# Modulations of the first layer by tiles of features, the first three products tile by tile, and the last modulation group by halves of columns

## The reference

```
def first_block(x, c, w_ada, b_ada, ...):
    c_act = jax.nn.silu(c)
    for i in range(DEPTH):
        mods = jnp.split(c_act @ w_ada[i] + b_ada[i], 6, axis=-1)
        sh1, sc1, g1, sh2, sc2, g2 = [m[:, None, :] for m in mods]
        u = x * (1.0 + sc1) + sh1
        ... y = gla_mixer(u, ...) or chunk_attention(u, ...)
        x = layer_norm(DEEPNORM_ALPHA * x + (1.0 + g1) * y, ...)
        u = x * (1.0 + sc2) + sh2
        y = squared_relu_mlp(u, ff_w1[i], ff_w2[i])
        x = layer_norm(DEEPNORM_ALPHA * x + (1.0 + g2) * y, ...)

def gla_mixer(u, w_in, w_gk2, b_gk, g_norm, w_out):
    proj = u @ w_in
    q, k, v, g, gk_lr = jnp.split(proj, ...)
    log_a = jax.nn.log_sigmoid((gk_lr @ w_gk2 + b_gk)) / GLA_GATE_TAU
    ... cumulated in chunks of 64 frames; q and k are scaled by its exponentials
```

## Time and profile before

| | us |
|---|---|
| median of 3 runs | 1144.07 (1142.17 to 1144.33) |
| the profiled execution, as timed | 1143.43 |
| its span in the trace | 1141.1 |
| PE busy | 1032.3 (90%) |
| DVE busy | 824.7 (72%) |
| ACT busy | 504.7 (44%) |
| all of PE's first 34.3 us | idle |

### The profile page before, as it was taken

One profiled execution on the slowest core, in us unless ns is written; L12 is line 12 of the kernel. 1 busy time (PEld: TensorE's weight loads), 2 busy tenths in 40 slices (PEclk: granted clock), 3 DMA queues, 4 the chain that ended last, 5 costly groups with the idle time before them and its releaser, 6 DMA issues. The chain is left out here.

```text
span 1141.1 us, 16510 instructions
## 1 busy us (share of the span) xinstructions
PE 1032.3 (90%) x6736; PEld 923.4 (81%) x6736; DVE 824.7 (72%) x1118; ACT 504.7 (44%) x669; POOL 64.1 (6%) x138
## 2 busy tenths in 40 slices
PE   0789988999999899868999999699999989999996
PEld 0778967899989688747898989488888879999995
DVE  4668898888779788747856556856876567777775
ACT  0464524333433644535334343354345555555553
POOL 3001110000000111100000000100000000000000
PEclk9989998999999999988999999799999999999999
DMA  9858775778778377322655555253343434555651
GB/s 340 334 197 302 276 298 196 287 291 304 283 275 320 105 289 247 129 74 74 240 189 180 195 177 197 89 170 138 111 144 116 148 130 152 200 171 186 198 172 68
DMA packets 35049, 227.91 MB, mean 200 GB/s; under 512 B 4096, under 2 KB 4224, under 8 KB 10144
## 3 DMA queue, kind: packets, MB, share of 16 engines
q1 hardware_dynamic: 25232, 167.01, 42.0%
q0 software_dynamic: 9744, 59.87, 14.0%
HBM read 225.82 MB, written 1.05 MB: 199 GB/s over the span
## 5 line engine op out<-in xcount | busy, mean ns | idle before, releaser
L1387 DVE TENSOR_TENSOR weight_lo<-weight_raw,weight_hi 128x2048 fp32r<-128x2048 f32 (+3 forms) x187 | 361.4, 1936 | 115.1 <-ACT weight_hi L991 115.0
L416 PE MATMUL ps<-act_hi,weight_hi 128*128 128x256 f32 x1400 | 354.2, 291 | 11.4 <-ACT gla_q L995 5.6
L991 ACT ACTIVATE weight_hi<-weight_raw 128x2048 fp32r<-128x2048 f32 (+2 forms) x168 | 299.9, 1786 | 128.9 <-PE ps L416 97.3
L416 PE MATMUL ps<-act_lo,weight_hi 128*128 128x256 f32 x1400 | 349.0, 287 | 0.0
L416 PEld LDWEIGHTS ps<-act_hi,weight_hi 128*128 128x128 f32 x1400 | 274.4, 196 | 23.0 <-issue 13.4
L416 PEld LDWEIGHTS ps<-act_lo,weight_hi 128*128 128x128 f32 x1400 | 274.7, 196 | 3.4 <-issue 1.0
L416 PE MATMUL ps<-act_hi,weight_lo 128*128 128x256 f32 x1400 | 186.8, 283 | 0.0
L416 PEld LDWEIGHTS ps<-act_hi,weight_lo 128*128 128x128 f32 x1400 | 175.5, 191 | 0.2
L1407 DVE SCALAR_TENSOR_TENSOR ada_acc<-ada_raw,c_act,ada_acc 128x2048 f32<-128x2048 f32 x42 | 98.6, 2349 | 10.2 <-DMA ada_raw<-ada 8.8
L416 PE MATMUL ps<-weight_hi,mlp_lo 128*128 128x512 f32 x256 | 101.8, 398 | 0.0
L416 PE MATMUL ps<-weight_hi,mlp_hi 128*128 128x512 f32 x256 | 101.6, 397 | 0.0
(11 more groups left out here) (311 smaller groups left out, 1263.0 us busy)
## 6 DMA issues: line engine op xcount, KB each, us to landing
weight_raw<-weights SPq DMA_DIRECT2D x144, 1024.0 KB, 5.0
ada_raw<-ada POOLq DMA_DIRECT2D x48, 1024.0 KB, 6.5
weight_raw<-weights SPq DMA_DIRECT2D x23, 512.0 KB, 3.6
row_g<-ln_rows POOLq DMA_DIRECT2D x4, 512.0 KB, 5.4
row_b<-ln_rows POOLq DMA_DIRECT2D x4, 512.0 KB, 7.7
att_bias<-rel_bias POOLq DMA_DIRECT2D x16, 128.0 KB, 3.5
square<-ada_rows POOLq DMA_DIRECT2D x3, 512.0 KB, 3.8
dev<-x_in SPq DMA_DIRECT2D x1, 1024.0 KB, 10.5
```

What stands on the lines that cost most here:

```text
L416: return e.matmul(o, a, b, start=start, stop=False, skip_group_check=True)
L991: e.activation(weight_hi[h][:, 0:size], weight_raw[r][:, 0:size], ACT.Copy).then_inc(hi_full[h], 1)
L1387: ins = e.tensor_tensor(weight_lo[h][:, c], weight_raw[r][:, c], weight_hi[h][:, c].bitcast(F32), ALU.subtract)
```

## The change

On the host (`_ada`), group 0 is stored by tiles of output features: chunk `f` holds all 1024 input features by 256 columns, the shift and scale of tile `f`. `first_input` on DVE runs eight accumulations of 256 columns per chunk and puts between them the reading of the modulations of the tile before (`mods_in`) and its `act_lo` (`residue`); the first three `split_lo` stand between tiles. PE sums a tile with one-column matmuls (`first_mods`), runs `gk` from tile 4 on and `q0` from tile 6 on, and then all of `q1` into a bank of its own, ahead of the gate products. ACT forms each tile's `act_hi` and `square` (DVE formed half of the latter before). SP no longer waits to load `x`, and loads the first weights after tiles 0, 2 and 4.

Groups 2 and 5 (the last of each layer) come by halves of columns: the first four chunks complete the 1024 columns of the MLP's scale, the last four those of its gate row; each chunk is two operations of 1024 columns. The scale then needs 20 chunks instead of 24: one chunk fewer after the third gate product, none before the mixer's output product, and four more in the first MLP. Both MLPs' gate rows are summed after block 8 instead of block 1.

```
-USES = ["m0", "gk", "q0", "q1", "k0", "k1", "v0", "v1", "v2", "v3", "g0", "g1", "g2", "sh0", "g3", "ra0", "ra1", "sc0"]
-USES += [f"up0_{i}" for i in range(2)] + ["rb0", "rb1"] + [f"up0_{i}" for i in range(2, 16)] + ["m3"]
+USES = ["gk", "q0", "k0", "k1", "v0", "v1", "v2", "v3", "g0", "g1", "g2", "sh0", "g3", "ra0", "ra1", "sc0"]
+USES += [f"up0_{i}" for i in range(9)] + ["rb0", "rb1"] + [f"up0_{i}" for i in range(9, 16)] + ["m3"]
...
-ACC_FREE = (0, 0, 1, 4, 7, 8)
-ADA_V, ADA_G = (1, 2, 2, 1), (2, 2, 2, 0)
+SUMS = ["sh0", "ra0", "ra1", "sc0", "rb0", "rb1", "m3", "sh1", "rc0", "rc1", "sc1", "rd0", "rd1"]
+ACC_FREE = (0, 0, 0, 3, 6, 7)
+ADA_V, ADA_G = (1, 2, 2, 1), (2, 2, 1, 0)
...
-            e.wait_ge(ada_used, 3)
...
-                    e.wait_ge(ada_used, 5 + j)
+                    e.wait_ge(ada_used, (1, 3, 5)[j])
...
-            def pair(one, two, ready, share=3, hook=None):
...
+            def first_mods(f):
+                e.wait_ge(ada_used, f + 1)
+                if f >= 2:
+                    e.wait_ge(u_mods, f - 1)
+                for x in range(2):
+                    last = e.matmul(ps[:, 6 + f % 2, x:x + 1], ada_acc[:, (2 * f + x) * P:(2 * f + x + 1) * P],
+                                    ones_sq[:, 0:1], start=(x == 0), stop=True, skip_group_check=True)
+                last.then_inc(u_summed, 1)
+            def first_chunk(j, outs, wide, tiles):
+                at = products(j, outs, act_hi, act_lo, KT, wide, True, False)
+                e.wait_ge(hi_full[j], 1)
+                e.wait_ge(lo_full[j], 1)
+                for k in tiles:
+                    e.wait_ge(lo_in, LO_U + k + 1)
+                    for n in range(len(outs)):
+                        o, one, two, three, start = at(n, k)
+                        mm(o, *one, start=start)
+                        mm(o, *two)
+                        last = mm(o, *three)
+                return last
...
-                if w >= 2:
-                    e.wait_ge(*emptied(w))
-                e.wait_ge(ada_used, KT * (group + 1))
+                e.wait_ge(*emptied(w))
+                e.wait_ge(ada_used, KT * (group + 1) - (4 if group % 3 == 2 else 0))
...
-            mods_of("m0", 0, 0, 16)
-            e.wait_ge(*emptied(W["q0"]))
-            pair((0, work_tiles(W["gk"], 1), P), (1, work_tiles(W["q0"]), 256), lambda k: (lo_in, LO_U + k + 1), share=6)
+            first = ((0, work_tiles(W["gk"], 1), P, 4), (1, work_tiles(W["q0"]), 256, 6))
+            for f in range(KT):
+                first_mods(f)
+                for j, outs, wide, begin in first:
+                    if f >= begin:
+                        first_chunk(j, outs, wide, range(f) if f == begin else (f - 1,))
+            for j, outs, wide, _ in first:
+                first_chunk(j, outs, wide, (KT - 1,)).then_inc(chunk_done, 1)
+            first_chunk(2, [(q1_ps[:, n, :], 4) for n in range(2)], 256, range(KT)).then_inc(chunk_done, 1)
             e.wait_ge(*evacuated(W["gk"]))
             e.wait_ge(w2_in, 16)
             for h in range(GLA_H):
                 last = e.matmul(gate_ps[:, h, :], g_w2[:, h * P:(h + 1) * P], g_gk[0:GLA_RANK, :], start=True, stop=True,
                                 skip_group_check=True)
             last.then_inc(gate_done, 1)
-            project(2, W["q1"])
...
-                if row:
-                    mod_row(row[0] + "0", row[1], D)
-                    mod_row(row[0] + "1", row[1], D + HALF)
                 for i in range(2, n_blocks - 1):
                     down(i - 2)
                     project(up_chunk(m, i), up_use(m, i))
+                    if row and i == 8:
+                        mod_row(row[0] + "0", row[1], D)
+                        mod_row(row[0] + "1", row[1], D + HALF)
...
-            split_hi(0)
-            split_hi(1)
-            e.wait_ge(scale_in, 1)
             e.wait_ge(x_arrived, 16)
             for k in range(KT):
                 scale, bias = norm_scale[:, 0, k:k + 1], mod(0, 0, k)
+                e.wait_ge(u_mods, k + 1)
                 e.activation(act_hi[:, k, :], dev[:, k, :], ACT.Identity, bias=bias, scale=scale).then_inc(hi_in, 1)
-                if k % 2:
-                    e.activation(square[:, k, :], dev[:, k, :], ACT.Identity, bias=bias, scale=scale).then_inc(hi_in, 1)
-            split_hi(2)
+                e.activation(square[:, k, :], dev[:, k, :], ACT.Identity, bias=bias, scale=scale).then_inc(hi_in, 1)
+                if k in (2, 4, 6):
+                    split_hi(k // 2 - 1)
...
-            evacuate(2, W["q1"], g_q[:, 2:4, :], halves(W["q1"]), GLA_DK ** -0.5)
+            e.wait_ge(chunk_done, 3)
+            e.activation(g_q[:, 2:4, :], q1_ps, ACT.Copy, scale=GLA_DK ** -0.5).then_inc(q1_in, 1)
...
-                    e.wait_ge(c_done, 1)
+                    e.wait_ge(u_summed, KT)
                     if ACC_FREE[n // KT]:
                         e.wait_ge(mods_summed, ACC_FREE[n // KT])
-                    ins = e.tensor_scalar(a, ada_raw[slot][:, :], c_act[:, 0:1], None, ALU.mult)
                 else:
                     e.wait_ge(ada_used, n)
-                    ins = e.scalar_tensor_tensor(out=a, in0=ada_raw[slot][:, :], scalar=c_act[:, k:k + 1], in1=a,
-                                                 op0=ALU.mult, op1=ALU.add)
+                if n // KT % 3 == 2:
+                    half = a[:, k // 4 * D:(k // 4 + 1) * D]
+                    parts = [(half, raw[:, x * D:(x + 1) * D], 2 * (k % 4) + x) for x in range(2)]
+                else:
+                    parts = [(a, raw[:, :], k)]
+                for x, (to, of, row) in enumerate(parts):
+                    if x:
+                        e.wait_ge(dve_step, own.of(ins))
+                    if row == 0:
+                        ins = e.tensor_scalar(to, of, c_act[:, 0:1], None, ALU.mult)
+                    else:
+                        ins = e.scalar_tensor_tensor(out=to, in0=of, scalar=c_act[:, row:row + 1], in1=to, op0=ALU.mult,
+                                                     op1=ALU.add)
...
-            def input_u():
...
+            def first_input():
+                def mods_in(f):
+                    b = VEC["b_ada"] + f
+                    e.wait_ge(u_summed, f + 1)
+                    n = own.of(e.tensor_tensor(mods[0][:, f:2 * KT:KT], ps[:, 6 + f % 2, 0:2], vec[:, b:b + KT + 1:KT],
+                                               ALU.add))
+                    e.wait_ge(dve_step, n)
+                    e.tensor_scalar(norm_scale[:, 0, f:f + 1], mod(0, 1, f), 1.0, None, ALU.add).then_inc(u_mods, 1)
+                def residue(f):
+                    e.wait_ge(hi_in, 2 * f + 2)
+                    e.tensor_tensor(act_lo[:, f, :], square[:, f, :], act_hi[:, f, :].bitcast(F32),
+                                    ALU.subtract).then_inc(lo_in, 1)
+                e.wait_ge(c_done, 1)
+                for f in range(KT):
+                    slot = f % N_ADA_RING
+                    to = ada_acc[:, 2 * f * P:2 * (f + 1) * P]
+                    raw = ada_raw[slot][:, :].rearrange("p (k n) -> p k n", k=KT)
+                    e.wait_ge(ada_full[slot], 16 * (f // N_ADA_RING + 1))
+                    n = own.of(e.tensor_scalar(to, raw[:, 0, :], c_act[:, 0:1], None, ALU.mult))
+                    for k in range(1, KT):
+                        e.wait_ge(dve_step, n)
+                        ins = e.scalar_tensor_tensor(out=to, in0=raw[:, k, :], scalar=c_act[:, k:k + 1], in1=to,
+                                                     op0=ALU.mult, op1=ALU.add)
+                        if k < KT - 1:
+                            n = own.of(ins)
+                            if f and k == 2:
+                                mods_in(f - 1)
+                            if f and k == 6:
+                                residue(f - 1)
+                    ins.then_inc(ada_used, 1)
+                    if f in (3, 5):
+                        split_lo(f // 2 - 1)
+                mods_in(KT - 1)
+                split_lo(2)
+                residue(KT - 1)
...
-            for _ in range(KT):
-                ada_chunk()
-            split_lo(0)
-            split_lo(1)
-            mods_of("m0", 0, 0, 16)
-            e.wait_ge(*evacuated(W["m0"]))
-            e.tensor_scalar(norm_scale[:, 0, :], mod(0, 1), 1.0, None, ALU.add).then_inc(scale_in, 1)
-            e.wait_ge(scale_in, 1)
-            e.wait_ge(x_arrived, 16)
-            input_u()
-            split_lo(2)
+            ada_at[0] = KT
+            first_input()
...
-            for _ in range(3):
-                ada_chunk()
...
-                for n in range(2):
-                    gate_half(f"{row}{n}", 2 * m + 1, n)
...
-                    if fill and i == n_blocks - 2:
+                    if i == 8:
+                        for n in range(2):
+                            gate_half(f"{row}{n}", 2 * m + 1, n)
+                    if fill and (i == n_blocks - 2 or i in (2, 4, 6, 10)):
...
```

(3 more changed lines are left out.)

78 lines of the change are left out of this document (19 added, 59 removed).

## The result

The changed kernel takes 1154.13 us, median of 4 runs (1152.73 to 1154.62); the kernel before, beside it, 1143.55 (1142.17 to 1144.33). The ratio is 1.0086, 95% interval 1.0063 to 1.0109: slower by 10.6 us in the medians, 9.7 in the profiled executions (span 1150.8 against 1141.1). The forecast was 1149.3 with a range of 1143.5 to 1155.0, slower at 0.77. The direction and the stated range held; the size was forecast at half, and 1154.13 lies outside the range that the forecast gave its own sum, 1146.5 to 1152.5.

A forecast was written before the change was run, and what follows sets the result against it. PE, busy 90% of the time, was taken to be held in the first stage by when the gate products are read. 6.6 - 1.3 - 0.4 + 0.3 = +5.2 us on 1143.43 gave 1148.6, as median 1149.3; range 1143.5 to 1155.0.

The forecast's parts named there:

- What counts is the read of the gate products: First stage: DVE's read of the gate products sets what follows, `k1`'s rounding 13.09 us behind; read at 62.2, before 55.13.
- DVE's tiles: First stage on DVE: first chunk at 9.8, 4.3 us a tile, tile 7 accumulated at 47.4, last residue done at 53.3.
- Rival B: First stage: small DVE operations follow at 0.40 us although they wait, a tile takes 3.6; 1142.1 us, chance 0.10.
- PE behind the last residue: First stage on PE: 9 matmuls 1.1 us, 48 of `q1` 5.8, gate products 2.0, read at 62.2; stage costs 6.6.
- given back 0.5: At `k1` on PE: it no longer waits for `q1`'s bank to be read, a gain of 0.5 us.
- The gate products' stage: One DVE chunk of 2.4 us goes ahead of PE's waits, halves add 1.1: a gain of 1.3 us.
- The layer norm: Behind the output product: three chunks leave DVE, so its lag behind PE goes, a gain of 0.4 us.
- The first MLP: Four more DVE chunks, 9.4 us, cost 0 under cover; the moved gate row's wait adds 0.3 us.
- The attention: Second layer: group 5's halves add 0.1 us to each chunk, under other work; nothing in the total.
- Rival D: PE's clock low through the burst and at `q1`, 1.6 to 2 us each, late chunks: +9 to +11, 1154, chance 0.13.
- C: Half mild first stage: first chunk near 7.6, PE's clock risen before the burst; +1.4, 1145.5 us, chance 0.15.
- E: Gate products' stage: the later gain does not come, PE finds another last wait; +6.5, 1150.6 us, chance within main forecast's 0.62.

The follow-up runs named there:

- E3: The changed kernel with the 48 products of `q1` put behind the gate products on PE; 1146.96 us, ratio 1.0019.
- E9: E8 with the fifth chunk, second half's sums and gate products' read taken earlier, and weight and residue roundings moved between later chunks; 1143.80 us, ratio 0.9970.
- E10: The changed kernel with `q1` behind the gates, last residue and gate read ahead of the third and fourth weight roundings, group 5 whole; 1143.24 us, ratio 0.9970.
- E11: E9 with 30 of `q0`'s 48 products put behind the gate products and ACT reading `q0`'s bank behind three gate steps; 1139.30 us, ratio 0.9951.
- E12: E7 with DVE reading the gate products ahead of rounding the fourth weight chunk, without tiles; 1141.43 us, ratio 0.9980 against the kernel before.
- E5: The changed kernel with tiles taken in pairs on DVE, so each operation waits for the one before the last; 1171.95 us.
- E7: The kernel before with only the second part: group 2 by halves, chunks and gate row moved, group 5 whole; 1143.20 us, ratio 0.9989.
- E1: The changed kernel with its second part undone, groups 2 and 5 whole, only the tiled first stage left; 1152.40 us, ratio 1.0082.
- E6: The changed kernel with the load of `x` held back until the first chunk of modulation weights has landed; 1153.04 us.
- E2: The changed kernel with group 5 accumulated over whole columns again, group 2 still by halves; 1152.96 us, ratio 1.0083.
- E4: The changed kernel with 6 or 7 extra products of ones on PE behind the sums of tiles 1 to 5; 1152.84 us.
- E8: The changed kernel with group 0 in two halves, 16 operations of 1024 columns, `q1` behind the gate products, group 5 whole; 1144.37 us, ratio 0.9994.

## Why the prediction was right in sign and half in size

**What counts is the read of the gate products: right.** In the changed kernel, E3, E9, E10, E11 and E12 the read stood at 63.69, 58.71, 55.50, 55.39, 51.59 and 53.43, and ACT's rounding of `k1`'s weights 13.08 to 13.10 behind it each time (13.09 in the forecast).

**DVE's tiles: right.** First chunk 9.2 for 9.8, a tile 4.25 for 4.3, last tile 46.9 for 47.4, its modulations 50.1, last residue 53.0 for 53.3. Rival B went by the Trainium skill, "VectorE: DVE Perf Modes", section "The DRAIN you can't avoid", which measured eight `tensor_copy` with a semaphore after each and says: "the semaphore costs nothing extra here". For the multiply-adds of this kernel the trace does not agree: in E5 the wait for the neighbour costs 0.12 us of 0.52, and B falls. The forecast also weighed a formula of the same page of the Trainium skill, (N+151)/0.96 in the section on the TRN2 errata. It is stated there for a float32 `tensor_tensor`, and for those it agrees: the subtractions of 256 columns took 420 to 430 ns for its 424. The multiply-adds are another operation and took 480, as in the forecast's sum. E10 shows that the sum's largest block, DVE's time, makes up little of the loss: 0.3 us against the kernel before, 2.0 against E12.

**PE behind the last residue: the step that failed in the first stage.** The forecast let PE run the last nine products and `q1` at 0.12 a product and had the gate products read at 62.2; 0.21 for 16 products there was only the range's upper end. It was so for those nine and the first eight of `q1`: 1.5 us, read at 63.7. And of "given back 0.5" 0.4 came (PE resumes 2.04 us behind the start of `k1`'s rounding, 2.43 in the kernel before), but the forecast had no price for the level behind the idleness: PE ran `k1` for 5.2 us at the low level (3.5 in the kernel before), which cost 0.7. So 0.3 was added where 0.5 was to be taken. Together 2.3 us: 8.9 for 6.6.

**The gate products' stage: mechanism right, size 0.9 for 1.3,** with 0.83 to 0.93 in all twelve traces that have this part. Mis-sized was the halves' cost, set at 1.1. In E7's rows the first chunk costs 0.78 more, the next two 0.52, and the fourth 0.25 (2.60 for 2.35), 1.55 in all, and 2.4 less 1.55 is 0.9.

**The layer norm: 0.5 for 0.4, by another cause.** The forecast took 0.45 us of DVE's lag behind PE away. The lag is still there in the changed kernel (PE's last product ends at 187.95, DVE takes it at 188.40), and E1, which keeps the three chunks, shows the same 0.45 as the others. Seven more traces show 0.45 to 0.47, and four show nothing (E3, E6, E10, E11). In these four the granted clock falls within 1 us of the operations at which it falls in the kernel before; in the others 2 us behind them or not at all. PE's eight products with `ident` in the layer norm, in the kernel before and in the changed one, show where the time went:

```profile
184.40 1.97 PE L523 MATMUL ps<-ident,dev 128*128 128x128 f32 x8 [1.61 <-DVE dev L1548]
```

```profile
192.36 1.09 PE L524 MATMUL ps<-ident,dev 128*128 128x128 f32 x8 [1.61 <-DVE dev L1565]
```

They take 1.97 us also in E3 and E10, which gain nothing. So it is a piece of low level that went, and not DVE's lag; that it went by chance, and not by something that the change did, was not tested. The forecast's 0.4 came true by luck.

**The first MLP: mechanism right, number by luck.** No wait for `hid_lo` came, and the gate row's wait, 0.36, is 0.9 now, its bound. The shift grows by 0.1 only for a forecast of 0.3, since two things meet: on PE's own operations 0.47 comes back at the first products (7.50 to 7.03), where the kernel before is at the low level until 190.3 and this execution is not, and the gate row adds 0.56.

**The attention: the other step that failed.** "Halves add 0.1 to each chunk, under other work": they add 0.25 to each and 1.0 to the first two together, and DVE is what PE waits for there: 2.0 us for 0, shown by E2 against the five kernels with halves. The forecast read the waits of PE to 290 us and took the second layer to be as covered as the first MLP; PE's wait for `att_s`, 3.3 us in the kernel before, would have told.

**Sum:** 8.9 - 0.9 - 0.5 + 0.1 - 0.4 (second norm) + 2.1 (attention) + 0.4 (behind) = 9.7, against 5.2. Rival D had named the low level at `q1` and 1154, but the burst was not low to its end, `k1` was not in it, and its late chunks did not come; its number was met in part through the attention, which it did not have. C and E fall: no part of the first stage was mild, and the later gain came.

## What to carry to other kernels

When a step is handed on in pieces so that the next engine can start early, look at what stands in that engine's queue between the last piece and the result that the rest waits for: here 48 products ahead of the gate products cost 5 us at that point, and the order of three steps of DVE another 3.3 (58.71 to 55.39). Where PE idles ahead of a critical block, price the block at the low level for its first microseconds, and count idleness removed as a second gain. An engine's small extra cost per operation is free only in the stages in which PE does not wait for it; look at those waits for every stage that the edit reaches, to the last layer.

## What the runs showed of the hardware that was not expected

**Idleness and the low level go together.** PE's wait ahead of `k1`, and for how long the granted clock is at 0.50 around it: 9.2 us idle, 10 us low (changed kernel, E1, E2, E4, E5, E6); 5.6 idle, 6.8 low (before, and E7); 5.2 idle, 6.8 low (E8); 3.9 idle, 6.9 low (E12); 3.5 idle, 6.9 low (E9) and 3.5 low (E10); 2.1 and 0.6 idle, not low (E3, E11).

**The granted clock in the record can say 1.00 at the low level.** Until its first change the column stands at 1.00: in E9 at 44 to 46 us with products 0.21 apart. In the changed kernel it says so at 44 to 46, and the spacing goes from 0.21 to 0.12 at 46.4. The spacing of like products is the surer sign (0.21 and 0.12 for 256 columns).

**The sums of one column are not cheaper.** Sixteen instructions took 1.95 us with one column in E8 and 1.95 us with 128 in the kernel before, at full level. At the low level they took 3.54 with one column in E8; with 128 it was 3.3, half of the 6.56 of the earlier trace rows, whose last 0.7 us were at the full level.

**Low stretches come and go between executions where the code is the same,** at 162, 182 to 202 and 502 to 510 us, and move the shift by 1.0 to 2.7 us each (1.0 in E12, 2.7 in E1): as much as most edits here.
